# Gate and up products of a feed-forward layer by Strassen's scheme on one Trainium2 core: seven block products in place of eight

## Chip, cores and metric

The kernel runs on one core of one Trainium2 chip. The metric is the device time of one launch in microseconds. The core's engines are TensorE (PE, with its weight loads as PEld), VectorE (DVE), ScalarE (ACT), GpSimd (POOL) and SyncE (SP, which issues the DMAs).

## What is computed

Two transformer blocks of different kinds on a sequence of 512 tokens by 1024 features, in float32. The first block has two layers, and the change lies in the second half of each of them:

```python
h2 = rmsnorm(x, norm_ffn[l])
gu = jnp.einsum('btd,df->btf', h2, w_gate_up[l])      # 1024 -> 2 * 2816
g, up = jnp.split(gu, 2, axis=-1)
x = x + jnp.einsum('btf,fd->btd', jax.nn.silu(g) * up, w_down[l])
```

`rmsnorm` divides by the root of a token's mean square and multiplies by a gain per feature. Ahead of it in the layer stand the input projection, a sliding-window attention, a convolution branch and `w_out`, whose product is added to `x`.

## The kernel before

Activations lie with features on the 128 partitions and the 512 tokens along the free dimension, so `x` is eight tiles of 128x512 (`KT` = 8). `FF` = 2816 gives `FT` = 22 output tiles of gate and 22 of up. TensorE gets close to float32 by splitting each operand into a high part (a ScalarE copy to float32r) and a low part (a VectorE subtraction, source minus high), and `mm3` issues three matmuls for each product: high by high, low by high, high by low.

Weights come as chunks of 128x2048 float32 (1 MB) by SyncE into `w_raw`, which has two slots. `prep` of ScalarE (L523) makes `w_hi` of a whole chunk and `prep` of VectorE (L1071) makes `w_lo`. One chunk serves one pair of gate and up tiles: `pair` on TensorE computes the gate tile in PSUM bank `mm0` and the up tile in `mm1`, 8 contraction tiles x 3 matmuls of 128x512 each, 48 matmuls a pair and 22 pairs a layer. `gated` on VectorE takes both banks with the factor `rstd` (L1082, the token's inverse root), ScalarE applies SiLU (L777), VectorE multiplies (L1407) and the product is split into `act_hi` (L546) and `act_lo` (L1100) for the down product, 8 output tiles of 22 x 3 matmuls.

Ahead of gate and up, the `w_out` stage makes the eight tiles of `x`. For each, VectorE adds the bank to `x` (L1382), ScalarE makes `in_hi` and a square, VectorE makes `in_lo` (L1105), and GpSimd adds the square to `ssum` (L464) for the norm. The sum over partitions is two matmuls (`sum_halves`) inside the first pair; ScalarE then makes `rstd`.

The order on each engine is written out by hand. Engines wait for one another by counting semaphores; the layers and the pairs are hardware loops on every engine, with registers for the counts.

Of the kernel before, what the change touches and what calls it, by code (L numbers as in the profile page):

```python
# [54 lines left out]
SIGMOID = "sigmoid_and_others"  # L55

# [4 lines left out]
L_MM = 102  # L61
# [74 lines left out]
def program(nc, W, X, CONST, PARL, PARS, ROPE1, ROPE2, SGT, DIST, GOUT, OUT, strides):  # L136
    with ExitStack() as ctx:
# [43 lines left out]
        xh = sb("in_hi", [P, KT, T], F32R)  # L181
        xl = sb("in_lo", [P, KT, T], F32R)
        acth, actl = phase(("act_hi", [P, FT, T], F32R), ("act_lo", [P, FT, T], F32R))
        (ga, y, apad, qr, _, kd, _, va, _, pr, pt, _, rope1) = phase(
# [113 lines left out]
        s_one = sem("ones_ready")  # L298

# [37 lines left out]
        def _(e):  # L337
            L = Loops(e, "sp", strides)
            w_free, raw_q, k_in, k_turned = (L.count(s) for s in (s_w, s_qr, s_kr, s_kt))

# [37 lines left out]
            with L.loop(0, DEPTH) as l:  # L378
# [3 lines left out]
                e.wait_ge(s_in, l * (2 * KT) + KT)  # L382
# [21 lines left out]
                stage(n + (10 + QT), (L_UG + L_KV + L_QG + L_GB + L_CO + L_OUT + L_GU - 10 - QT) // 2)  # L404
                stage(n + (L_CHUNKS - L_DOWN), L_DOWN // 2, (HALF, HALF))
# [43 lines left out]
        def _(e):  # L449
# [3 lines left out]
            guess, scale = L.count(s_qx), L.count(s_qn)  # L453
            e.sem_inc(s_sum, 2)
# [35 lines left out]
            with L.loop(0, DEPTH) as l:  # L490
# [5 lines left out]
                add_squares()  # L496
                add_squares()
# [3 lines left out]
        def _(e):  # L501
# [6 lines left out]
            root, gel, par, r2 = L.count(s_rs), L.count(s_gel), L.count(s_par), L.count(s_r2)  # L508
            ogs, raw_q, means, guess, dens = (L.count(s) for s in (s_og, s_qr, s_hm, s_qx, s_rl))
# [139 lines left out]
            with L.loop(0, DEPTH) as l:  # L649
# [106 lines left out]
                with L.loop(0, L_OUT // 2) as i:  # L756
                    for c in range(2):
                        for d in range(2):
                            m = i * 4 + (2 * c + d)
                            tiles.skip(1)  # L760
                            if d:
                                prep(c)
                            e.wait_ge(s_sum, added.next())
                            e.wait_ge(s_mmf, taken.next())
                            hi(tile(xh, m), tile(x, m), col(parl, m + A_GF))
                            square(tile(x, m), d)
# [3 lines left out]
                inverse_root(tD[:], rstd[:])  # L770


                def gated(m, c, cols=CH):
                    tiles.skip(2)
                    prep(c, cols)
                    e.wait_ge(s_mmf, taken.next())
# [1639 lines left out]
```

## Time and profile before

| | |
|---|---|
| median of 3 runs | 2195.36 us (2194.89 to 2195.74) |
| the profiled execution | 2195.25 us, its span 2193.5 us |
| TensorE busy | 2181.2 us, 99% of the span |
| VectorE busy | 1377.9 us, 63% |
| ScalarE busy | 965.3 us, 44% |
| GpSimd busy | 74.8 us, 3% |
| gate and up, each layer | 240.2 us |

Matmuls are pipelined: the row of one shows from its start to its modelled end, and the next one starts before that. The rate of a stream is the distance from one start to the next. The same holds, to a smaller degree, for instructions of VectorE and ScalarE that stand back to back.

### The profile page before, as it was taken

The numbers are of one execution on the slowest core, as the hardware profiler recorded it, in microseconds if no ns is written. First come the engines' busy times: TensorE is split into PE (matmuls) and PEld (weight loads), VectorE is DVE, ScalarE is ACT, GpSimd is POOL, SyncE is SP. The second block draws the span as 40 slices with busy tenths as digits, with TensorE's granted clock in tenths as the row PEclk, the third lists the DMA queues.
The fourth block names the chain that finished last, engine by engine and source line by source line (L and its number), as shares of the span: only waits on it lengthen the run. The fifth ranks groups of instructions, "written<-read, shape, count | busy, mean of one in ns | idle before, by whom it ended". The sixth has DMA issues, their size and how long they took to land.

```text
span 2193.5 us, 28930 instructions
## 1 busy us (share of the span) xinstructions
PE 2181.2 (99%) x10528; PEld 1812.7 (83%) x10528; DVE 1377.9 (63%) x1978; ACT 965.3 (44%) x1392; POOL 74.8 (3%) x103
## 2 busy tenths in 40 slices
PE   9999999999999999999999999999999999999998
PEld 6878888888888878888888888888888899888887
DVE  8999944444335999954444334654776568888723
ACT  5678444443223588544343223332554344333412
POOL 0000020000010000020000010000000000000000
PEclk9999999999999999999999999999999999999999
DMA  5221222222223211222222224223222231222222
GB/s 188 69 81 61 97 96 96 96 96 84 93 94 122 90 62 65 94 96 99 98 98 94 81 92 152 100 78 128 82 96 88 97 135 39 103 99 99 92 96 77
DMA packets 35653, 208.39 MB, mean 95 GB/s; under 512 B 4512, under 2 KB 5024, under 8 KB 15072
## 3 DMA queue, kind: packets, MB, share of 16 engines
q1 hardware_dynamic: 35120, 206.43, 27.0%
q8 instruction: 60, 0.98, 0.2%
q10 hardware_dynamic: 432, 0.64, 0.1%
q14 instruction: 41, 0.34, 0.0%
HBM read 201.15 MB, written 2.10 MB: 93 GB/s over the span
## 4 chain that ended last, share of the span: by engine, by line
PE 94%; ACT 3%; DVE 2%; issue 1%; DMA 0%; SPq 0%; DVEq 0%; ACTq 0%
PE mm L1797 25%; PE mm L1799 25%; PE mm L1798 25%; PE sp L1799 4%; PE sp L1798 4%; PE sp L1797 4%; PE sp L1899 1%; PE ob L1927 1%; ACT probs L582 1%; DVE conv_y L1172 1%; DVE probs L1202 1%; ACT probs L590 1%; PE sp L1914 0%; DMA x<-in_x_dram 0%; PE ob L1799 0%
## 5 line engine op out<-in xcount | busy, mean ns | idle before, releaser
L1797 PE MATMUL mm<-in_hi,w_hi 128*128 128x512 f32 (+1 forms) x1696 | 663.5, 391 | 3.2 <-DVE w_lo L1071 1.6
L1799 PE MATMUL mm<-in_hi,w_lo 128*128 128x512 f32 (+1 forms) x1696 | 657.0, 387 | 0.0
L1798 PE MATMUL mm<-in_lo,w_hi 128*128 128x512 f32 (+1 forms) x1696 | 656.9, 387 | 0.0
L523 ACT ACTIVATE w_hi<-w_raw 128x2048 fp32r<-128x2048 f32 (+3 forms) x193 | 346.2, 1794 | 674.4 <-PE mm L1799 557.2
L1071 DVE TENSOR_TENSOR w_lo<-w_raw,w_hi 128x2048 fp32r<-128x2048 f32 (+3 forms) x193 | 422.2, 2188 | 240.2 <-ACT w_hi L523 239.8
L1797 PEld LDWEIGHTS mm<-in_hi,w_hi 128*128 128x128 f32 x1696 | 318.4, 188 | 74.4 <-issue 8.0
L1799 PEld LDWEIGHTS mm<-in_hi,w_lo 128*128 128x128 f32 x1696 | 318.4, 188 | 65.4
L1798 PEld LDWEIGHTS mm<-in_lo,w_hi 128*128 128x128 f32 x1696 | 318.6, 188 | 64.2 <-issue 1.0
L1172 DVE SCALAR_TENSOR_TENSOR conv_y<-conv_in,parl,conv_y 128x512 f32<-128x512 f32 x240 | 169.9, 746 | 1.7
L1082 DVE TENSOR_TENSOR tB<-mm,rstd 128x512 f32<-128x512 f32 x54 | 37.3, 690 | 172.8 <-PE mm L1799 172.8
L1797 PE MATMUL mm<-act_hi,w_hi 128*128 128x512 f32 x352 | 136.9, 389 | 0.0
L1798 PE MATMUL mm<-act_lo,w_hi 128*128 128x512 f32 x352 | 136.9, 389 | 0.0
L1799 PE MATMUL mm<-act_hi,w_lo 128*128 128x512 f32 x352 | 136.9, 389 | 0.0
L1797 PE MATMUL sp<-in_hi,w_hi 128*128 128x512 f32 (+1 forms) x256 | 96.8, 378 | 0.0
L1799 PE MATMUL sp<-in_hi,w_lo 128*128 128x512 f32 (+1 forms) x256 | 96.2, 376 | 0.0
L1798 PE MATMUL sp<-in_lo,w_hi 128*128 128x512 f32 (+1 forms) x256 | 96.2, 376 | 0.0
L464 POOL TENSOR_TENSOR ssum<-ssum,sq 128x512 f32<-128x512 f32 x28 | 54.8, 1957 | 881.4 <-ACT sq L549 881.4
L546 ACT ACTIVATE act_hi<-tD 128x512 f32 (+1 forms) x66 | 41.4, 628 | 87.9 <-DVE tD L1407 80.4
L1798 PEld LDWEIGHTS mm<-act_lo,w_hi 128*128 128x128 f32 x352 | 66.1, 188 | 13.8
L1797 PEld LDWEIGHTS mm<-act_hi,w_hi 128*128 128x128 f32 x352 | 66.1, 188 | 13.6
L1799 PEld LDWEIGHTS mm<-act_hi,w_lo 128*128 128x128 f32 x352 | 66.1, 188 | 13.6
L1100 DVE TENSOR_TENSOR act_lo<-tD,act_hi 128x512 f32 (+1 forms) x66 | 45.5, 689 | 41.1 <-ACT act_hi L546 41.1
(429 smaller groups left out, 3251.5 us busy)
## 6 DMA issues: line engine op xcount, KB each, us to landing
w_raw<-in_w_dram SPq DMA_DIRECT2D x160, 1024.0 KB, 4.8
w_raw<-in_w_dram SPq DMA_DIRECT2D x32, 704.0 KB, 3.9
w_raw<-in_w_dram SPq DMA_DIRECT2D x5, 512.0 KB, 4.5
out_dram<-z_rows SPq DMA_DIRECT2D x8, 256.0 KB, 2.1
rope<-in_rope_dram SPq DMA_DIRECT2D x3, 512.0 KB, 3.7
x<-in_x_dram SPq DMA_DIRECT2D x4, 256.0 KB, 4.8
x<-in_x_dram SPq DMA_DIRECT2D x2, 512.0 KB, 8.3
sq<-ssum SPq DMA_DIRECT2D x32, 32.0 KB, 1.8
```

The lines of the kernel that those rows point to most:

```text
L464: e.tensor_tensor(ssum[:], ssum[:], sq[:, k % 2, :], ALU.add).then_inc(s_sum, added.up())
L523: e.activation(whi[:, slot, 0:cols], raw[:, slot, 0:cols], ACT.Copy).then_inc(s_whi, whi_out.up())
L546: e.activation(dst, src, ACT.Copy, scale=scale).then_inc(s_fn, fn.up())
L582: last = e.activation(p, p, ACT.Exp, bias=ng[:, j:j + 1], accum_out=ls[:, j:j + 1])
L590: last = e.activation(p, p, ACT.Copy, scale=rl[:, 4 * h + n:4 * h + n + 1])
L1071: TT(wlo[:, slot, first:cols], raw[:, slot, first:cols], r32(whi[:, slot, first:cols]), ALU.subtract).then_inc(s_w, w_out.up())
L1082: TT(dst, four[bank], rstd[:] if op_in is None else op_in, ALU.mult).then_inc(s_mmf, taken.up())
L1100: TT(dst, src, r32(hi_), ALU.subtract).then_inc(told.sem, told.up())
L1172: STT(y[:, t, :], a, w, y[:, t, :], ALU.mult, ALU.add).then_inc(s_do, own.up())
L1797: MM(out, ah, bh, start=first, stop=False, **kw)
L1798: MM(out, ah, bl, start=False, stop=False, **kw)
L1799: return MM(out, al, bh, start=False, stop=last, **kw)
```

## The change

Gate and up of one tile are seen as a 2x2 block product: the rows of blocks are gate and up, the contraction of 1024 is cut in two halves of 512, and the 512 tokens are cut in two halves of 256. Winograd's form of Strassen's scheme gives the four result blocks from seven block products, each of 4 contraction tiles x 3 matmuls of 128x256: 84 of them for a pair. For this it needs

- four sums of token blocks (`T1` to `T4`), made once per layer while the `w_out` stage runs, with high and low parts of seven token operands of 4 tiles each;
- four sums of weight blocks (S1, S2, S4 and W21-W11) for every pair, three by GpSimd (`weight_sums`) and one by VectorE (`fourth_sum`), with high and low parts of seven weight operands of 128x512, each in its own `spot` of `w_hi` and `w_lo`;
- partial results that are used twice: ScalarE copies three half banks a pair out of PSUM (`copied_out`) and VectorE adds them to other banks (`take_product`).

The up half is no longer multiplied by `rstd`; in its place `down` multiplies its result by `rstd` before it is added to `x`. The first `KEPT` = 12 activation tiles lie where the first token operands also lie, so they are kept in float32 and split only at the end of the stage. The down product takes the tiles in the order 12 to 21, then 0 to 11. The loops of VectorE, ScalarE and GpSimd over layers and pairs are written out. TensorE still loops. The pieces of the diff are, in this order, GpSimd's, ScalarE's, VectorE's and TensorE's, and last the line of `down` on VectorE.

```diff
+    def weight_sums(a, fifth_done):
+        e.wait_ge(s_raw[a], raws[a].next(16))
+        e.wait_ge(s_sm, done.now(-fifth_done))
+        e.tensor_tensor(spot(wsum, 1), raw[:, a, A21], raw[:, a, A22], ALU.add).then_inc(s_su, made.up())
+        e.wait_ge(s_sm, done.now(-3))
+        e.wait_ge(s_su, made.now())
+        e.tensor_tensor(spot(wsum, 2), raw[:, a, A11], spot(wsum, 1),
+                        ALU.subtract).then_inc(s_su, made.up())
+        e.wait_ge(s_sm, done.now(-6))
+        e.tensor_tensor(spot(wsum, 4), raw[:, a, A21], raw[:, a, A11],
+                        ALU.subtract).then_inc(s_su, made.up())
+        done.skip(7)
...
-    def gated(m, c, cols=CH):
-        tiles.skip(2)
-        prep(c, cols)
-        e.wait_ge(s_mmf, taken.next())
-        e.activation(tC[:], tA[:, 0:T], ACT.Silu).then_inc(s_fn, fn.up())
-        taken.skip(1)
-        e.wait_ge(s_val, val.next())
-        hi(tile(acth, m), tD[:])
+    def gated_pair(p, m, split):
+        silu()
+        e.wait_ge(s_su, summed.next())
+        high_of_sum(4)
+        copied_out(copy_5[p % 2], bank_z[p % 2], 1)
+        e.wait_ge(s_sm, done.now(-2))
+        high_of(6, raw[:, p % 2, A22])
+        if split:
+            act_high(m)
+        copied_out(copy_2[p % 2], bank_x[p % 2], 3)
+        if p < FT - 1:
+            next_weights(p)
+            if p < FT - 2:
+                weights_beyond(p)
+            done.skip(7)
...
-    def gated(m, c, cols=CH):
-        take(tA[:, 0:T], 0)
-        take(tB[:, 0:T], 1)
-        prep(c, cols)
-        e.wait_ge(s_fn, fn.next())
-        e.wait_ge(s_mmf, taken.now())
-        TT(tD[:], tC[:], tB[:, 0:T], ALU.mult).then_inc(s_val, val.up())
-        lo(tile(actl, m), tD[:], tile(acth, m))
+    def gated_pair(p, m, split):
+        low_of_sum(4)
+        act_of(p - 1, m, 2, val if split else own, fn.next())
+        low_of(6, raw[:, p % 2, A22])
+        if split:
+            act_low(m)
+        upper_takes(p, 4)
+        lows_for_next(p)
+        lower_takes(p, (6, 7), p < FT - 2)
...
+            def gated_pair(p):
+                a = p % 2
+                e.wait_ge(s_sv, products.now(5))
+                operand(3)
+                times(bank_z[a], 1, T1, True)
+                e.wait_ge(s_sv, products.now(2))
+                times(bank_x[1 - a], 6, T4, False)
+                e.wait_ge(s_sc, copies.now(-1))
+                operand(4)
+                times(bank_x[a], 2, T2, False)
+                e.wait_ge(s_sv, products.now(3))
+                times(bank_y, 3, B21, True)
+                last = p == FT - 1
+                if not last:
+                    e.wait_ge(s_sv, products.now(0))
+                    operand(6)
+                    times(bank_x[1 - a], 0, B11, True)
+                e.wait_ge(s_sc, copies.now(-3))
+                operand(6 if last else 7)
+                times(bank_x[a], 4, T3, False)
+                e.wait_ge(s_sc, copies.now(-2))
+                operand(5)
+                times(bank_z[a], spot_s4(p), B22, False)
...
-                    TT(tile(x, m), mm[d][:], tile(x, m), ALU.add).then_inc(s_mmf, taken.up())
+                    scaled = (tA, tB)[d][:, 0:T]
+                    TT(scaled, mm[d][:], rstd[:], ALU.mult).then_inc(s_mmf, taken.up())
+                    e.wait_ge(s_mmf, taken.now())
+                    TT(tile(x, m), scaled, tile(x, m), ALU.add).then_inc(s_val, val.up())
```

Below, the seven products of a pair are called P1 to P7 in TensorE's order: T1 by S1, T4 by W22 (which ends the pair before), T2 by S2, B21 by W12, B11 by the next pair's W11, T3 by W21-W11, B22 by S4.

This is one pair of tiles on VectorE in the loop of gate and up, before (`mm` is a PSUM bank, the names after the arrow are inputs):

```order
839 L1082 TENSOR_TENSOR tA<-mm,rstd 128x512 [waits tile_ready]
840 L1081 REGISTER_ALU
841 L1082 TENSOR_TENSOR tB<-mm,rstd 128x512 [waits tile_ready]
842 L1070 ISA
843 L1071 TENSOR_TENSOR w_lo<-w_raw,w_hi 128x2048 [waits w_hi_ready]
844 L1405 ISA
845 L1406 ISA [waits scalar_value]
846 L1407 TENSOR_TENSOR tD<-tC,tB 128x512 [waits tile_taken]
```

And this is one pair on VectorE after, from the middle of the stage (`sp` is PSUM too, `sq` and `tD` hold ScalarE's copies):

```order
468 L1606 TENSOR_TENSOR w_lo<-w_raw,w_hi 128x512 [waits weight_operand_high]
469 L1687 TENSOR_TENSOR tA<-sp,tD 128x256 [waits product_copied,strassen_product_ready]
470 L1606 TENSOR_TENSOR w_lo<-w_raw,w_hi 128x512 [waits weight_operand_high]
471 L1672 TENSOR_TENSOR w_sum<-w_raw,w_sum 128x512 [waits weight_sum_by_pool]
472 L1606 TENSOR_TENSOR w_lo<-w_sum,w_hi 128x512 [waits weight_operand_high] x3
473 L1687 TENSOR_TENSOR tB<-mm,sq 128x256 [waits product_copied,strassen_product_ready]
474 L1687 TENSOR_TENSOR tA<-sp,sq 128x256 [waits product_copied,strassen_product_ready]
475 L1692 TENSOR_TENSOR tA<-tA,rstd 128x512 [waits product_taken]
476 L1606 TENSOR_TENSOR w_lo<-w_raw,w_hi 128x512 [waits weight_operand_high]
477 L1606 TENSOR_TENSOR w_lo<-w_sum,w_hi 128x512 [waits weight_operand_high]
478 L1698 TENSOR_TENSOR act<-mm,tC 128x256 [waits strassen_product_ready,scalar_value]
479 L1699 TENSOR_TENSOR act<-tB,tC 128x256
```

Four instructions and a split of the activation have become fourteen, and the split of the activation is a fifteenth where the tile is not kept.

On GpSimd nothing stood between the seven additions of squares of the `w_out` stage and those of the down stage. After, three sums for each of 21 pairs stand there:

```order
45 L530 TENSOR_TENSOR ssum<-ssum,sq 128x512 [waits square_ready,sum_zeroed]
46 L530 TENSOR_TENSOR ssum<-ssum,sq 128x512 [waits square_added,square_ready] x6
47 L571 TENSOR_TENSOR w_sum<-w_raw 128x512 [waits strassen_product_ready,raw_loaded1]
48 L574 TENSOR_TENSOR w_sum<-w_raw,w_sum 128x512 [waits weight_sum_by_pool,strassen_product_ready]
49 L577 TENSOR_TENSOR w_sum<-w_raw 128x512 [waits strassen_product_ready]
```

In the `w_out` stage VectorE had, for each tile of `x`, the addition and `in_lo`. After, this stands there for the sixth and the start of the seventh tile:

```order
426 L1606 TENSOR_TENSOR w_lo<-w_raw,w_hi 128x512 [waits weight_operand_high]
427 L1649 TENSOR_TENSOR w_sum<-w_raw 128x512
428 L1651 TENSOR_TENSOR w_sum<-w_raw,w_sum 128x512 [waits weight_sum_by_vector]
429 L1653 TENSOR_TENSOR tA<-w_raw,w_sum 128x512 [waits weight_sum_by_vector]
430 L1606 TENSOR_TENSOR w_lo<-w_sum,w_hi 128x512 [waits weight_operand_high] x2
431 L1606 TENSOR_TENSOR w_lo<-w_raw,w_hi 128x512 [waits weight_operand_high]
432 L1614 TENSOR_TENSOR x<-mm,x 128x512 [waits tile_ready]
433 L1630 SCALAR_TENSOR_TENSOR early<-early,parl,tB 128x256 [waits scalar_value]
434 L1631 SCALAR_TENSOR_TENSOR in_sum<-x,parl,tB 128x256
```

The first pair's weight work has moved ahead of the seventh tile's addition, and each of the last four tiles brings eight instructions of 128x256 in place of one of 128x512.

## Rows read from the trace of the kernel before

**Rows 1.** The page's busy times and instruction counts by engine.

```profile
PE 2181.2 (99%) x10528; PEld 1812.7 (83%) x10528; DVE 1377.9 (63%) x1978; ACT 965.3 (44%) x1392; POOL 74.8 (3%) x103
```

**Rows 2.** Busy time by stretch: `w_out`, gate and up, and down of layer 0.

```profile
core 0: us, PE busy (x) PEld busy (x) DVE busy (x) ACT busy (x) POOL busy (x), PEclk, DMA share, GB/s
272.10:315.60 43.50, 43.50 (x193) 36.03 (x192) 21.73 (x23) 17.01 (x20) 15.56 (x7) 1.00 0.29 104
315.60:555.80 240.20, 240.19 (x1060) 198.59 (x1060) 108.54 (x113) 96.94 (x90) 0.00 (x0) 1.00 0.27 92
555.80:675.70 119.90, 119.81 (x529) 98.92 (x527) 44.82 (x35) 31.82 (x33) 11.83 (x7) 1.00 0.29 96
```

**Rows 3.** Timeline: start, duration; first and 42nd matmul of a stream of 128x256.

```profile
1776.55 0.28 PE L1797 MATMUL mm<-in_hi,w_out 128*128 128x256 f32 x1
...
1781.40 0.28 PE L1799 MATMUL mm<-in_hi,w_out 128*128 128x256 f32 x1
```

**Rows 4.** Timeline of VectorE in gate and up; brackets: idle before, and releaser.

```profile
536.16 2.29 DVE L1071 TENSOR_TENSOR w_lo<-w_raw,w_hi 128x2048 fp32r<-128x2048 f32 x1 [1.26 <-ACT w_hi L523]
...
545.09 0.69 DVE L1082 TENSOR_TENSOR tB<-mm,rstd 128x512 f32<-128x512 f32 x1 [3.80 <-PE mm L1799]
546.50 1.62 DVE L1071 TENSOR_TENSOR w_lo<-w_raw,w_hi 128x1408 fp32r<-128x1408 f32 x1 [0.72 <-ACT w_hi L523]
```

**Rows 5.** Timeline of VectorE, instructions back to back in another stage.

```profile
250.26 0.69 DVE L1360 TENSOR_TENSOR conv_lo<-conv_y,conv_hi 128x512 fp32r<-128x512 f32 x1
250.87 0.68 DVE L1100 TENSOR_TENSOR conv_lo<-conv_y,conv_hi 128x512 fp32r<-128x512 f32 x1
...
253.28 0.69 DVE L1082 TENSOR_TENSOR tC<-mm,gate_b 128x512 f32<-128x512 f32 x1 [1.13 <-PE mm L1799]
254.01 0.69 DVE L1374 TENSOR_TENSOR tD<-tC,gate_a 128x512 f32<-128x512 f32 x1
```

**Rows 6.** VectorE by line and form: count, busy us, mean ns, idle before.

```profile
L1661 DVE TENSOR_TENSOR ssum<-ssum,sq 128x256 f32<-128x256 f32 x24 | 9.9, 417 | 0.3 <-ACT sq L954 0.3
L1679 DVE SCALAR_TENSOR_TENSOR in_lo<-x,pars,in_hi 128x256 fp32r<-128x256 f32 x16 | 7.6, 478 | 0.2 <-ACT in_hi L546 0.2
```

**Rows 7.** ScalarE by line and form, the same columns.

```profile
L546 ACT ACTIVATE act_hi<-tD 128x512 f32 x60 | 37.6, 627 | 78.7 <-DVE tD L1407 73.3 <-DVE tD L1738 5.4
L777 ACT ACT_TABLE_LOAD x20 | 25.7, 1283 | 0.4
L546 ACT ACTIVATE rv_hi<-og 128x256 fp32r<-128x256 f32 x16 | 5.7, 402 | 0.0
```

**Rows 8.** Timeline of VectorE at two additions of GpSimd.

```profile
286.43 2.28 DVE L1071 TENSOR_TENSOR w_lo<-w_raw,w_hi 128x2048 fp32r<-128x2048 f32 x1
288.64 0.69 DVE L1382 TENSOR_TENSOR x<-mm,x 128x512 f32<-128x512 f32 x1
...
603.01 0.75 DVE L1105 SCALAR_TENSOR_TENSOR in_lo<-x,parl,in_hi  x1 [1.35 <-ACT in_hi L546]
603.68 2.72 DVE L1071 TENSOR_TENSOR w_lo<-w_raw,w_hi 128x1408 fp32r<-128x1408 f32 x1
```

**Rows 9.** Timeline of GpSimd, these two additions.

```profile
286.41 3.45 POOL L464 TENSOR_TENSOR ssum<-ssum,sq 128x512 f32<-128x512 f32 x1 [4.18 <-ACT sq L549]
...
603.52 1.40 POOL L464 TENSOR_TENSOR ssum<-ssum,sq 128x512 f32<-128x512 f32 x1 [13.21 <-ACT sq L549]
```

**Rows 10.** Timeline of VectorE in the `w_out` stage: tiles 5, 6 and 7 of `x`.

```profile
304.96 0.69 DVE L1382 TENSOR_TENSOR x<-mm,x 128x512 f32<-128x512 f32 x1 [3.01 <-PE mm L1799]
...
310.40 0.69 DVE L1382 TENSOR_TENSOR x<-mm,x 128x512 f32<-128x512 f32 x1
...
315.84 0.69 DVE L1382 TENSOR_TENSOR x<-mm,x 128x512 f32<-128x512 f32 x1 [3.01 <-PE mm L1799]
```

**Rows 11.** The page's DMA issues: KB each, us from issue to landing.

```profile
w_raw<-in_w_dram SPq DMA_DIRECT2D x160, 1024.0 KB, 4.8
```

**Rows 12.** Longest of TensorE's waits, 33 to 315 us: total, times, longest.

```profile
PE sp L1914 <- ACT probs L590: 0.8, 3, 0.3
```

More of the change, by code:

```diff
@@ L55 @@
 SIGMOID = "sigmoid_and_others"
+SILU = "silu_and_others"
 L_UG, L_KV, L_QG, L_GB, L_CO, L_OUT, L_GU, L_DOWN = 4, 2, 8, 4, 2, 4, 22, 16
@@ L489, in _ @@
             added.skip(KT)
-            with L.loop(0, DEPTH) as l:
+            for l in range(0, DEPTH):
                 e.wait_ge(s_mmf, l * L_MM + 2)
@@ L647, in _ @@
             sum_hi()
-            with L.loop(0, DEPTH) as l:
+            for l in range(0, DEPTH):
                 e.preload_act_table_set(LN_EXP)
@@ L767, in _, with high_of, high_of_sum, copied_out @@
-                sum_hi()
+                def high_of(n, src):
+                    e.activation(spot(whi, n), src, ACT.Copy).then_inc(s_sh, high.up())
+                def high_of_sum(n):
+                    high_of(n, spot(wsum, n))
+                def copied_out(dst, src, product):
+                    e.wait_ge(s_sm, done.now(-product))
+                    e.activation(dst, src, ACT.Copy).then_inc(s_sc, copies.up())
+                def landed(slot):
+                    e.wait_ge(s_raw[slot], raws[slot].next(16))
@@ new lines, in token_high, with first_weights, first_sums @@
+                def token_high(o, k, src, scale=1.0):
+                    hi(token_operand(HIGH, o, k), src, scale)
+                def first_weights():
+                    landed(0)
+                    e.wait_ge(s_mm, tiles.now())
+                    high_of(0, raw[:, 0, A11])
+                def first_sums():
+                    for n in (1, 2):
+                        e.wait_ge(s_ds, sums.next())
+                        high_of_sum(n)
+                    high_of(3, raw[:, 0, A12])
@@ L782, in _, with prep_down @@
-                with L.loop(0, L_GU // 2 - 1) as i:
-                    gated(i * 2, 0)
-                    gated(i * 2 + 1, 1)
-                gated(FT - 2, 0, HALF)
-                gated(FT - 1, 1, HALF)
+                inverse_root(tC[:], rstd[:])
+                weights_beyond(0)
+                e.preload_act_table_set(SILU)
+                for p in range(1, FT):
+                    gated_pair(p, p - 1, p > KEPT)
+                def prep_down(slot, product):
+                    landed(slot)
+                    e.wait_ge(s_sm, done.now(-product))
+                    e.activation(whi[:, slot, 0:HALF], raw[:, slot, 0:HALF], ACT.Copy).then_inc(s_whi, whi_out.up())
@@ L937, in _ @@
                 ret_gate(2 + d, 1, d)
-            with L.loop(1, S_AR // 2) as i:
+            for i in range(1, S_AR // 2):
                 for c in range(2):
@@ L1174, in convolve @@
                 at[0] += count
-            with L.loop(0, DEPTH) as l:
+            for l in range(0, DEPTH):
                 input_norm(ems, zero=False)
@@ L1429, in down @@
                         prep(1, cols)
-                with L.loop(0, KT // 2 - 1) as i:
+                for i in range(0, KT // 2 - 1):
                     down(i * 2, 0)
@@ L1636, in _ @@
                 ret_gate(2 + d, 1, d)
-            with L.loop(1, S_AR // 2) as i:
+            for i in range(1, S_AR // 2):
                 for c in range(2):
@@ L1879, in two, with times @@
                         ins.then_inc(s_mm, tiles.up())
-                two(sub)
+                two((kept, sub))
                 with L.loop(1, KT // 2):
                     two(None)
+            def times(out, n, o, start, ready=None):
+                for k in range(HK):
+                    if ready is not None:
+                        e.wait_ge(s_cmb, combos.now(-ready(k)))
+                    a = slice(k * P, k * P + P)
+                    ins = mm3(out, spot(whi, n)[:, a], spot(wlo, n)[:, a], token_operand(HIGH, o, k),
+                              token_operand(LOW, o, k), start and k == 0, k == HK - 1, skip_group_check=True)
+                ins.then_inc(s_sm, done.up())
```

390 lines of the change are left out of this document (337 added, 53 removed).

## The prediction, made before the changed kernel ran

> **What bounds the kernel now.** The page comes first: TensorE is busy for 99% of the span, VectorE 63%, ScalarE 44%, GpSimd 3% [rows 1]. The stretches then show where: gate and up of one layer take 240.20 us, TensorE is busy in all of it at full clock, GpSimd does nothing there, and VectorE is busy for 108.54 us, under half [rows 2]. So time is won here by fewer columns through TensorE, as long as the others keep up. The timeline of VectorE shows how much room they have: in a pair it is idle 3.80 us before it takes the up bank [rows 4]. Last I read how GpSimd and VectorE meet in the two other stages [rows 8, 9], since the change puts both to work at once.
>
> **What TensorE saves.** 1060 matmuls in 240.20 us are 0.2266 us each [rows 2], so a pair of 48 takes 10.88 us. Matmuls of 128x256 in a stream start every (1781.40 - 1776.55)/41 = 0.1183 us [rows 3]. 84 of them are 9.94 us. The saving is 0.94 us a pair, 20.7 us a layer, 41.4 us in all, if nothing else ends later. The Trainium skill (TensorE: Matmul & The Clock Gate, "Back-to-back issue gap") gives a gap of N/2.4 + 2.5 ns, so 0.216 and 0.109 us; by it a pair would go from 10.36 to 9.17 us and save 1.19. The rows are slower at both widths, and I use them.
>
> **What VectorE must do.** Back to back, instructions of 128x512 start 0.61 us apart; one that reads what the one before wrote starts 0.73 us after it [rows 5]. One of 128x256 takes 0.417 us [rows 6], and less the same overlap of 0.08 it starts 0.34 apart. A pair needs seven low parts, one weight sum and the gate times `rstd`, nine of 128x512, 5.61 us with one dependence, and five of 128x256 (three takes, two for the activation), 1.72 us: 7.33 us. Where the activation is split in the pair (8 of 20 pairs), 7.94. Both are below 9.94.
>
> **What GpSimd adds.** It makes three sums of 128x512 a pair. Its addition at 286.41 took 3.45 us: VectorE's `w_lo` held it to 288.71, and it ended at 289.86, so 1.15 us of its own [rows 8, 9]. The addition at 603.52 began to run when `in_lo` ended at 603.76 and ended at 604.92; `w_lo` behind it took 2.72 us [rows 8, 9] where the same form takes 1.62 [rows 4], so VectorE lost 1.10. The addition `x<-mm,x`, with one input from PSUM, ran its usual 0.69 us beside GpSimd [rows 8]. So they exclude each other wherever VectorE reads two SBUF tensors, which is ten of its fourteen instructions. The Trainium skill (SBUF — State Buffer, on the shared port pair) calls this an exclusive lock held for a whole instruction. It speaks against the change: by it, three sums in a row with no gap give 7.33 + 3.45 = 10.78 us a pair, where TensorE alone needs 9.94. The trace agrees with the lock, and what is left to find is how much of the 3.45 falls beside PSUM instructions or gaps.
>
> **One pair, laid out.** TensorE's products end at 1.6, 3.0, 4.4, 5.8, 7.3, 8.7 and 10.1 us after the pair's start (1.42 each, with the last matmul's 0.28). VectorE can't begin the gate times `rstd` until P7 is taken. Then SiLU 0.63, the high part of W21-W11 0.54 behind it (ScalarE's 0.63 less overlap) [rows 7], its low part and the activation follow, and P5 of the next pair waits for that activation's read of its bank. Two sums of GpSimd (after P1 and after P3) fall into this chain, the third (after P6) into the low parts that P1 of the next pair waits for. I laid instruction behind instruction in this order, GpSimd going first where it asked first. The first sum is half covered by the take from PSUM or the wait for SiLU, the second by the first half of the activation, the third costs all of its 1.15. Adding some 0.6 us in which VectorE waits for SiLU and the high part, in kept pairs VectorE comes round in 10.2 to 10.4 us: I take **10.3**. With the split, 0.61 more and a wait for its high part: 11.0 to 11.4, **11.2**. TensorE waits for VectorE in both. Weights come in time: a slot is free about 3 us before the pair ends and the load takes 4.8 us [rows 11], so it lands some 2 us into the next pair, where the first sum wants it at 1.6 and the high part of W11 only after.
>
> **The start.** Take tile 5's product as time 0 (304.93); tiles come every 5.44 us [rows 10] and gate and up would start at 10.7. Tile 5 brings 0.69, eight STT or TT of 128x256 (0.40 and 0.34 apart [rows 6]) and 0.55 of waiting for ScalarE, 4.4 us; the first weights 4.5 us; GpSimd's addition of the square 1.1. So tile 6 is added at 9.9 instead of 5.5, and tile 7 at 14.2 instead of 10.9. Its token operands, with one addition of GpSimd and the first weight sum in the way, are ready at about 19.0, where P3 would end at 15.0. P5 then waits for a low part that stands behind them, to 22.3. The first pair, with the 0.95 us of `sum_halves`, ends at about 27.5 where it could at 21.6. In the second pair stand, in series, take, mean square, logarithm and exponential (0.63 each), `rstd` times gate, a table load of 1.28 [rows 7], SiLU and the low part, before P5: 2.6 us more. Two pairs of before end at 10.7 + 22.7 = 33.4, two of after at about 40.1: **6.7 us lost** in each layer.
>
> **The rest.** The second instruction of `down` (0.73 us per tile of 15 us) and the 12 late splits (0.61 each on VectorE, 0.54 on ScalarE, while TensorE spends 0.68 on each tile) lie under the down product, in which VectorE is busy 44.82 of 119.90 us [rows 2]; uncovered, the last tile's would cost 0.7 us a layer. Loops without registers can give back little: the largest wait of TensorE in the attention is 0.8 us a layer [rows 12]. I put both at nothing. The last pair has no P5 of a next one and a weight split between: 10.4.
>
> **The sum**, for one layer: +6.7 at the start; 11 kept pairs x (10.3 - 10.88) = -6.4; 8 split pairs x (11.2 - 10.88) = +2.6; last pair -0.5. That is +2.4, in two layers +4.8 us. The profiled execution took 2195.25 us, 0.1 from the median of the runs, so **2200 us**. With 0.2 us either way on the pairs and 2 on the start this case spans 2188 to 2212. Within 0.2% (4.4 us) two times can't be told apart here.
>
> **The rivals.**
> - *TensorE stays the bound.* GpSimd finds room beside VectorE, pairs take 9.94, and the start loses 4.4 without GpSimd's share. 4.4 - 19 x 0.94 - 0.9 is -14.4 a layer: **2166**. For it: 7.94 us of VectorE's work in 9.94. Against it: the full 1.10 that VectorE lost at 603.68 [rows 8]. Chance 0.18.
> - *Sums mostly in gaps.* GpSimd's requests meet the waits for SiLU and for P4 and P6 more often than I laid out: pairs 10.1 and 10.7, start 6.2. 6.2 - 8.6 - 1.4 - 0.7 is -4.5 a layer: **2186**. Chance 0.20.
> - *My case*, **2200**, chance 0.40.
> - *The chain to P5 closes* (slower). If the second sum asks just before the low part of W21-W11 instead of just behind it, which in my layout is a matter of 0.1 us, the activation is read 0.9 us after P5 wanted its bank, and the pair becomes 10.9, split 11.65; from a pair of 10.88 on, nothing is won at all. With 8 lost at the start: 8 + 0.2 + 6.2 is +14.4 a layer: **2224**. Chance 0.22.
>
> **How the numbers follow.** Faster by over 0.2% are the first two: 0.38. My case lies across the bound of 2199.8 and I give 0.14 of its 0.40 to no change and 0.26 to slower; with the last rival, slower is 0.48. The range takes most of the first and last case: 2168 to 2224.
>
> **What would show it.** In the profile after: matmuls of 128x256 at 0.118 us apart within a product, with TensorE's waits between products, on `act` or `w_lo`; VectorE busy 75 to 80% of gate and up; GpSimd's sums of 1.2 to 1.8 us and `w_lo` of 128x512 stretched from 0.69 to about 1.8 beside them; P3 of the first pair waiting 3 to 5 us. If TensorE has no waits in the middle of the stage, the first rival is right. If the waits are before P5, the last; before P1 and P2, mine. I would be wrong altogether if 256-wide matmuls that change PSUM bank every twelve were slower than the stream in [rows 3], or if ScalarE, with 11 or 12 instructions a pair, came late.

## The result, and the profile after

The changed kernel takes 2200.45 us (median of 8 runs, 2198.94 to 2203.09) where the kernel before, run beside it, takes 2195.41 (2194.89 to 2195.80). The ratio is 1.0024, 95% interval 1.0015 to 1.0034: slower by a quarter of a per cent, although TensorE now has 9% less to do in gate and up. Its profiled execution took 2199.27 us, with a span of 2197.5.

The page of the changed kernel: the busy times to hold against [rows 1], the chain that ended last, and two groups of VectorE's low parts (line, form, count, busy us, mean ns, idle before).

```profile
PE 2157.3 (98%) x12112; PEld 1862.3 (85%) x12112; DVE 1657.0 (75%) x2512; ACT 1048.0 (48%) x1789; POOL 266.8 (12%) x229
...
PE 71%; DVE 17%; ACT 5%; issue 4%; DMA 2%; SPq 0%; DVEq 0%
...
L1606 DVE TENSOR_TENSOR w_lo<-w_sum,w_hi 128x512 fp32r<-128x512 f32 x174 | 156.3, 938 | 18.6 <-ACT w_hi L851 18.6
...
L1606 DVE TENSOR_TENSOR w_lo<-w_raw,w_hi 128x512 fp32r<-128x512 f32 x132 | 115.5, 875 | 5.5 <-ACT w_hi L851 5.5
```

A low part of 128x512 takes 0.69 us in the kernel before [rows 5], and 0.88 (from `w_raw`) and 0.94 (from `w_sum`) on average here. The gate-up stages of both layers, as busy time by stretch, the columns as in [rows 2]:

```profile
315.14:557.43 242.29, 228.38 (x1852) 223.67 (x1851) 226.77 (x335) 134.61 (x270) 100.51 (x64) 0.99 0.27 94
981.21:1224.43 243.22, 228.35 (x1851) 223.41 (x1851) 227.39 (x335) 134.91 (x270) 99.95 (x64) 0.99 0.26 94
```

Against 240.20 us [rows 2] that is 2.1 and 3.0 more, where TensorE alone would need some 20 less. VectorE is busy for 94% of the stage. What TensorE waited for in the middle of it, 340 to 555 us (total, times, longest):

```profile
PE mm L2158 <- DVE tB L1687: 4.9, 8, 0.6
PE mm L2158 <- DVE act L1698: 4.4, 4, 1.6
```

A kept pair is one whose activation tile stays in float32 for the time being, a split pair one in which it is split. All of these waits are for VectorE. Those for `tB` (the product that must be taken before P2) are 0.61 or 0.62 us each, in seven of the 8 split pairs and in the last pair. Those for `act` stand before P5: the longest, 1.6 us, still belongs to the second pair, which ends at 344.1, and the three others are 0.96 us each, in three kept pairs. The first matmuls of P1 in the timeline give the length of each pair. Of the 11 kept pairs eight take 9.94 to 10.17, and three, every third or fourth, take 11.4. Such a long pair, first on VectorE, then GpSimd, ScalarE and TensorE (timeline: start, us, and in brackets the idle time before and what ended it):

```profile
365.93 1.73 DVE L1692 TENSOR_TENSOR tA<-tA,rstd 128x512 f32<-128x512 f32 x1
367.59 0.68 DVE L1606 TENSOR_TENSOR w_lo<-w_raw,w_hi 128x512 fp32r<-128x512 f32 x1
368.88 1.76 DVE L1606 TENSOR_TENSOR w_lo<-w_sum,w_hi 128x512 fp32r<-128x512 f32 x1 [0.62 <-ACT w_hi L851]
370.56 0.41 DVE L1698 TENSOR_TENSOR act<-mm,tC 128x256 f32<-128x256 f32 x1
...
365.83 1.28 POOL L571 TENSOR_TENSOR w_sum<-w_raw 128x512 f32<-128x512 f32 x1 [1.16 <-DMA w_raw<-in_w_dram]
368.81 1.28 POOL L574 TENSOR_TENSOR w_sum<-w_raw,w_sum 128x512 f32<-128x512 f32 x1 [1.70 <-PE mm L2160]
...
367.69 0.63 ACT L945 ACTIVATE tC<-tA 128x512 f32<-128x512 f32 x1 [1.27 <-DVE tA L1692]
368.23 0.61 ACT L851 ACTIVATE w_hi<-w_sum 128x512 fp32r<-128x512 f32 x1
...
369.87 0.28 PE L2160 MATMUL sp<-early_hi,w_lo 128*128 128x256 f32 x1
371.11 0.38 PE L2158 MATMUL mm<-in_hi,w_hi 128*128 128x256 f32 x1 [0.96 <-DVE act L1698]
```

Read it as a chain. GpSimd's first sum stretches the gate times `rstd` from 0.69 to 1.73 us. SiLU on ScalarE waits for it, and the high part of W21-W11 waits behind SiLU, though its input, GpSimd's third sum, was ready at 364.7 us. VectorE is idle for 0.62 us until that high part comes at 368.85. By then GpSimd's second sum is 0.07 us ahead, and the low part takes 1.76 us. The activation is read that much later. P5 starts 1.24 us after the matmul before it, where 0.12 is the distance in a stream: 1.1 us late.

A split pair, of which all but the first last 10.95 to 10.97 us, has the same idle time and three stretched instructions:

```profile
481.92 1.05 DVE L1692 TENSOR_TENSOR tA<-tA,rstd 128x512 f32<-128x512 f32 x1
...
484.19 0.69 DVE L1606 TENSOR_TENSOR w_lo<-w_sum,w_hi 128x512 fp32r<-128x512 f32 x1 [0.61 <-ACT w_hi L851]
...
485.13 1.23 DVE L1699 TENSOR_TENSOR act<-tB,tC 128x256 f32<-128x256 f32 x1
...
489.21 2.98 DVE L1606 TENSOR_TENSOR w_lo<-w_sum,w_hi 128x512 fp32r<-128x512 f32 x3
```

The first sum costs VectorE 0.36 us here, the second 0.81, and the third, in one of the three low parts of the last row, 1.09.

### The profile page after: what moved, and what is told of

Its sections match the earlier page's. It is cut to its first block, busy times and chain, and to the rows that moved or that the text cites. A ratio compares the mean times of both kernels' runs of the same rounds, so it can differ in the third digit from the quotient of the medians.

```text
span 2197.5 us, 31630 instructions
## 1 busy us (share of the span) xinstructions
PE 2157.3 (98%) x12112; PEld 1862.3 (85%) x12112; DVE 1657.0 (75%) x2512; ACT 1048.0 (48%) x1789; POOL 266.8 (12%) x229
## 4 chain that ended last, share of the span: by engine, by line
PE 71%; DVE 17%; ACT 5%; issue 4%; DMA 2%; SPq 0%; DVEq 0%
PE mm L2158 18%; PE mm L2160 17%; PE mm L2159 17%; DVE w_lo L1606 7%; PE sp L2160 4%; PE sp L2158 4%; PE sp L2159 4%; DMA w_raw<-in_w_dram 2%; DVE act L1699 1%; DVE tA L1692 1%; DVE conv_y L1386 1%; DVE tA L1687 1%; DVE w_sum L1672 1%; ACT w_hi L851 1%; DVE probs L1416 1%
## 5 line engine op out<-in xcount | busy, mean ns | idle before, releaser
L2158 PE MATMUL mm<-in_hi,w_hi 128*128 128x512 f32 (+1 forms) x1520 | 545.3, 359 | 24.9 <-DVE tB L1687 11.2
L2159 PE MATMUL mm<-in_lo,w_hi 128*128 128x512 f32 (+1 forms) x1520 | 532.6, 350 | 0.0
L2160 PE MATMUL mm<-in_hi,w_lo 128*128 128x512 f32 (+1 forms) x1520 | 532.5, 350 | 0.0
L616 ACT ACTIVATE w_hi<-w_raw 128x2048 fp32r<-128x2048 f32 (+3 forms) x145 | 256.2, 1767 | 461.4 <-PE mm L2160 343.4
L1285 DVE TENSOR_TENSOR w_lo<-w_raw,w_hi 128x2048 fp32r<-128x2048 f32 (+3 forms) x149 | 323.2, 2171 | 195.9 <-ACT w_hi L616 193.5
L1606 DVE TENSOR_TENSOR w_lo<-w_sum,w_hi 128x512 fp32r<-128x512 f32 x174 | 156.3, 938 | 18.6 <-ACT w_hi L851 18.6
L1606 DVE TENSOR_TENSOR w_lo<-w_raw,w_hi 128x512 fp32r<-128x512 f32 x132 | 115.5, 875 | 5.5 <-ACT w_hi L851 5.5
L851 ACT ACTIVATE w_hi<-w_sum 128x512 fp32r<-128x512 f32 x174 | 104.3, 621 | 18.2 <-DVE w_sum L1672 10.9
L2158 PE MATMUL sp<-early_hi,w_hi 128*128 128x256 f32 x352 | 100.2, 285 | 0.0
L2159 PE MATMUL sp<-early_lo,w_hi 128*128 128x256 f32 x352 | 100.2, 285 | 0.0
```

Of the source, the lines that this page charges most:

```text
L616: e.activation(whi[:, slot, 0:cols], raw[:, slot, 0:cols], ACT.Copy).then_inc(s_whi, whi_out.up())
L851: e.activation(spot(whi, n), src, ACT.Copy).then_inc(s_sh, high.up())
L1285: TT(wlo[:, slot, first:cols], raw[:, slot, first:cols], r32(whi[:, slot, first:cols]), ALU.subtract).then_inc(s_w, w_out.up())
L1606: TT(spot(wlo, n), src, r32(spot(whi, n)), ALU.subtract).then_inc(s_so, operands.up())
L2158: MM(out, ah, bh, start=first, stop=False, **kw)
L2159: MM(out, ah, bl, start=False, stop=False, **kw)
```

## Experiments

Each kernel was timed against the kernel before on the same chip, which took 2195.1 to 2195.4 us throughout. Times of pairs are worked out from the starts of P1 in the timeline of layer 0 (kept and split: the mean). e2 and e11 don't compute the products and serve only as measurements.

| kernel | us | ratio to before, 95% | first two pairs | kept (11) | split (8) | last |
|---|---|---|---|---|---|---|
| changed | 2200.45 | 1.0015 to 1.0034 | 28.96 | 10.38 | 10.86 | 12.23 |
| e1 sums on VectorE | 2200.04 | 1.0014 to 1.0032 | 30.24 | 10.20 | 11.09 | 12.18 |
| e2 fills for sums | 2163.99 | 0.9843 to 0.9873 | 26.23 | 9.94 | 9.94 | 10.43 |
| e3 second sum later | 2216.93 | 1.0086 to 1.0117 | 30.49 | 10.89 | 11.22 | 12.23 |
| e4 before, no loops | 2193.88 | 0.9985 to 1.0003 | | | | |
| e8 e1 + high part first | 2178.59 | 0.9909 to 0.9936 | 29.81 | 9.94 | 10.30 | 11.05 |
| e5 e8 + sums earlier | 2170.51 | 0.9873 to 0.9904 | 27.88 | 9.96 | 9.98 | 11.03 |
| e6 e5 + start, end | 2170.21 | 0.9871 to 0.9901 | 28.45 | 9.96 | 9.98 | 10.11 |
| e7 changed + start, end | 2196.28 | 0.9997 to 1.0015 | 27.66 | 10.38 | 11.01 | 11.19 |
| e9 e5 + root early, end | 2163.89 | 0.9841 to 0.9871 | 25.95 | 9.94 | 9.98 | 10.11 |
| e10 changed + high part first | 2185.36 | 0.9941 to 0.9968 | 28.43 | 10.15 | 10.63 | 10.83 |
| e11 one-input sums | 2166.95 | 0.9858 to 0.9889 | 27.57 | 9.94 | 9.94 | 10.59 |
| e12 e9 + copy of P1 early | 2164.71 | 0.9845 to 0.9878 | 26.22 | 9.94 | 9.98 | 10.11 |

**What GpSimd's sums cost.** First they go to VectorE, then they are replaced by something that reads nothing.

```diff
 # e1, VectorE
                         act_low(m)
+                    first_sum(p + 1)
                     upper_takes(p, 4)
...
                     low_of(3, raw[:, (p + 1) % 2, A12])
+                    second_sum(p + 1)
                     fourth_sum(p)
...
                     take_product(tB[:, 0:TH], bank_x[p % 2], copy_5[p % 2], seventh, 2)
+                    third_sum(p + 1)
```

> The changed kernel with the three weight sums of each pair on VectorE (in their places between its own instructions) and none on GpSimd in the gate-up stage. Theory A (a sum on GpSimd and a VectorE instruction that reads two SBUF operands run one after the other, so each sum takes its own 1.2 us from VectorE and comes late by what VectorE has already queued): VectorE has 7.33 + 3 x 0.65 = 9.3 us to do in a kept pair and 9.9 in a split one, all its own, against TensorE's 9.94; kept pairs 9.95 to 10.1 us instead of 10.38, split pairs 10.0 to 10.4 instead of 10.87, no wait of 1.24 us before P5 in every third pair; 4 to 8 us less per layer, 2184 to 2192 us in all. Theory B (VectorE is at its limit by the number of its own instructions and their order, and GpSimd's sums are mostly in its gaps): three more instructions a pair add up to 2 us to each of 19 pairs per layer, 2215 us or more.

```diff
 # e2, GpSimd, all three sums
-                    e.tensor_tensor(spot(wsum, 1), raw[:, a, A21], raw[:, a, A22], ALU.add).then_inc(s_su, made.up())
+                    e.memset(spot(wsum, 1), 0.0).then_inc(s_su, made.up())
...
```

> The changed kernel, where GpSimd's three sums per pair are replaced by fills with zero of the same 512 columns, with the same waits and signals; the sums of weight blocks are left out, so gate and up are not computed. Theory A (the cost is the shared reading of SBUF by two-operand instructions): a fill reads nothing, VectorE's low parts beside it stay at 0.6 us each and no sum is late; kept pairs 9.94 us, split pairs 9.94 to 10.2, 2174 to 2184 us in all. Theory B (the waits before P5 and P2 come from VectorE's and ScalarE's own orders or from the landing of the weights, whatever GpSimd does): pairs as they are, 2196 to 2202 us.

e2 came out 10 us below the range of theory A. It took 36 us off the changed kernel, and every pair from the third to the one before the last ran in 9.94 us. The fill took 0.53 us, and no instruction of VectorE was stretched beside one. So GpSimd's sums hold the pairs up; a fill is also shorter than a sum (0.53 against 1.28 us), and e2 alone doesn't part that from the reading. e11 below narrows it down. But e1, which takes the sums off GpSimd too, won nothing, and neither theory had its number. VectorE by group in e1, 340 to 555 us (the last columns are the idle time before and its releaser):

```profile
L1582 DVE TENSOR_TENSOR w_lo<-w_sum,w_hi 128x512 fp32r<-128x512 f32 x80 | 51.6, 686 | 13.0 <-ACT w_hi L826 13.0
L1582 DVE TENSOR_TENSOR w_lo<-w_raw,w_hi 128x512 fp32r<-128x512 f32 x60 | 41.2, 686 | 7.2 <-ACT w_hi L826 7.2
```

No low part is stretched any more, but VectorE is idle for 20.2 us in these 20 pairs, 0.65 and 0.36 us in each, waiting for high parts of ScalarE. With 9.9 us of its own work (split) that makes 10.9 of the 11.09 measured. In e2 VectorE waits as long for the same high parts (12.7 and 6.4 us over the same stretch), but there it has three instructions less to do in a pair and makes up for it. The idle time costs only where VectorE is full.

**The same two edits, singly and together.** Two lines of ScalarE are swapped, in e1 (e8) and in the changed kernel (e10).

```diff
-                    silu()
                     e.wait_ge(s_su, summed.next())
                     high_of_sum(4)
+                    silu()
```

> The kernel with all three sums on VectorE, where ScalarE also makes the high part of W21-W11 ahead of the pair's silu and not behind it. In the run without this VectorE was idle 0.62 us a pair, waiting for that high part, 0.36 us for the high part of W12 and 0.1 to 0.2 us otherwise, on 9.3 us (kept) or 9.9 us (split) of its own work; periods of 10.30 and 11.09 us. If those waits are the rest of the period (VectorE's chain sets it): 9.94 us in kept pairs, 10.5 in split ones, 8 to 9 us less per layer, 2181 to 2185 us. If the period comes from the chain over TensorE's products and the copies, whatever VectorE's own waits: 2198 to 2202 us.

> The changed kernel, its sums on GpSimd, with ScalarE's high part of W21-W11 ahead of silu and nothing else: the edit that took 21 us from the kernel with its sums on VectorE. If GpSimd's sums are what holds VectorE up (it has no idle time before that low part in the changed kernel, since a stretched instruction stands ahead of it): 2198 to 2201 us, no change. If the place of the high part is what costs in the changed kernel too: kept pairs near 9.94 and split ones near 10.4, 2185 us or less.

e8 came out 2.4 us under its range, with kept pairs at 9.94 and split ones at 10.30. In e10 the second case came, 0.4 us above its bound and with longer pairs than it said, 10.15 and 10.63. The premise of the first case was wrong: VectorE does have idle time there, the 0.62 us in the rows above. The swap alone takes 15 us off, where moving all sums alone takes off 0.4.

| us | SiLU first | high part first |
|---|---|---|
| sums on GpSimd | 2200.45 | 2185.36 |
| sums on VectorE | 2200.04 | 2178.59 |

The timeline of e10 in the pair that answers to the one above:

```profile
365.94 1.73 DVE L1692 TENSOR_TENSOR tA<-tA,rstd 128x512 f32<-128x512 f32 x1
367.60 0.68 DVE L1606 TENSOR_TENSOR w_lo<-w_raw,w_hi 128x512 fp32r<-128x512 f32 x1
368.20 0.68 DVE L1606 TENSOR_TENSOR w_lo<-w_sum,w_hi 128x512 fp32r<-128x512 f32 x1
368.81 0.41 DVE L1698 TENSOR_TENSOR act<-mm,tC 128x256 f32<-128x256 f32 x1
369.14 1.25 DVE L1699 TENSOR_TENSOR act<-tB,tC 128x256 f32<-128x256 f32 x1
```

The first sum stretches the gate exactly as before, but the high part is there and the low part gets in ahead of the second sum, which now stretches the second half of the activation, behind the read that P5 waits for. That read comes at 368.81 and not at 370.56. The sums cost VectorE no less (54.8 us over 340 to 555 us, against 48.8 in the changed kernel, counted as under e11 below). What is gone is its idle time before this low part, and with it the waits before P5 of kept pairs; those before P2 shrink from 4.9 to 2.8 us.

**Where the second sum falls.**

```diff
 # e3, GpSimd, before the second sum
                     e.wait_ge(s_su, made.now())
+                    if q > 1:
+                        e.wait_ge(s_so, lows.now(-7 * q))
```

> The changed kernel, where GpSimd's second sum of each pair from the third on also waits until VectorE has finished the low part of W21-W11 of the pair before. If the waits of 1.24 us before P5 in every third kept pair come from the second sum asking less than 0.1 us ahead of that low part and holding it up: they vanish, kept pairs 10.0 to 10.2 us instead of 10.38, split pairs as before, 2190 to 2196 us. If they come from the landing of weights or from ScalarE: still there, 2199 to 2202. If the sum made later is itself late for the next P1 or P3: new waits there, 2202 or more.

The wait for `act` before P5 did vanish past the second pair, but the third outcome came: TensorE waited up to 0.6 us for `w_lo` before P1 in nine pairs of the layer and up to 0.6 for `tB` in ten, 2217 us. This run shows that this delay of GpSimd's sum is no cure: the sum is late for what follows it.

**Early sums.** e5 is e8 with VectorE's second and fourth sum ahead of the take of P4 and no longer between the low parts.

```diff
                     first_sum(p + 1)
+                    e.wait_ge(s_sm, done.now(-3))
+                    second_sum(p + 1)
+                    fourth_sum(p)
                     upper_takes(p, 4)
...
                     low_of(3, raw[:, (p + 1) % 2, A12])
-                    second_sum(p + 1)
-                    fourth_sum(p)
                     low_of_sum(1)
```

> As the run before, and VectorE also makes the second and the fourth sum ahead of taking the fourth product, so that it doesn't stand idle for the high part of W12. VectorE's chain sets the period: 0.36 us less in split pairs, 10.0 to 10.2 us against TensorE's 9.94, kept pairs 9.94; 2175 to 2179 us. If TensorE's products set it: the time of the run before, 2181 to 2185 or 2200. If the early sums make the take of the fourth product late and with it P4 and P5: 2185 or more.

2170.5, some 5 us under the range: it also gave 2 us a layer at the start, which I hadn't counted. VectorE's groups in e5, same stretch:

```profile
L1582 DVE TENSOR_TENSOR w_lo<-w_sum,w_hi 128x512 fp32r<-128x512 f32 x80 | 51.4, 684 | 0.0
L1582 DVE TENSOR_TENSOR w_lo<-w_raw,w_hi 128x512 fp32r<-128x512 f32 x59 | 40.3, 683 | 0.0
```

The 20 us that VectorE waited for high parts in e1 are gone (the swap took 13.0 of them, the early sums the rest), and with them TensorE's waits in this stretch but for 0.6 us.

**One input instead of two.** In e11 each sum on GpSimd reads one block.

```diff
-                    e.tensor_tensor(spot(wsum, 1), raw[:, a, A21], raw[:, a, A22], ALU.add).then_inc(s_su, made.up())
+                    e.tensor_scalar(spot(wsum, 1), raw[:, a, A21], 2.0, 0.0, ALU.mult, ALU.add).then_inc(s_su, made.up())
...
```

> The changed kernel, where each of GpSimd's sums reads one block only (twice that block, 512 columns, same waits and signals); the sums of weight blocks are left out, so gate and up are not computed. If what holds VectorE up is two instructions with two SBUF inputs each at once: VectorE's low parts stay at 0.6 us each and the time is that of the fills, 2164 to 2168 us. If any GpSimd instruction that reads SBUF holds it up: 2180 us or more, with low parts of 1.2 us or longer beside it.

The instruction of GpSimd takes 0.88 us on average, two thirds more than the fill. The time is that of the first theory, its reason is not quite: a VectorE instruction beside such a one still takes up to 1.10 us instead of 0.69. Over 340 to 555 us such excess (over 0.685 us for 128x512 and 0.417 for 128x256) is 9.7 us in 27 instructions, where it is 48.8 us in 58 in the changed kernel. There are 58 sums in both: VectorE loses 0.84 us on average to one with two inputs, 0.17 to one with one, and nothing to a fill (e2).

**Start and end.** e6 and e7 make the same edits to e5 and to the changed kernel: ScalarE copies the first product ahead of tile 7, the third sum stands behind tile 7, VectorE adds the last three squares itself, and at the end the product for P7 is taken ahead of the low parts for down.

```diff
                 upper_takes(FT - 1, 4)
-                prep(0, HALF)
...
-                kept_low(0)
                 take_product(tB[:, 0:TH], bank_x[1], copy_5[1], 5, 2)
+                prep(0, HALF)
                 take_product(tA[:, TH:T], bank_z[1], copy_2[1], 6, 3)
                 copies.skip(3)
                 scaled_gate()
+                kept_low(0)
                 kept_low(1)
```

> As the run before, with the start and the end of the stage changed too: at the start ScalarE copies the first product ahead of tile 7, VectorE makes the third sum behind tile 7 and adds the last three squares itself, so that GpSimd adds none beside it; at the end VectorE takes the product for P7 ahead of the low parts for down. If the wait of 2.5 us before P3 comes from the copy's place and the wait behind it from GpSimd's additions stretching VectorE: P3 begins 2 us earlier, 1.5 to 3 us less per layer; the end gives 1.0 us per layer. 2168 to 2173 us. If the start is bound by VectorE's own forms between tiles 6 and 7: only the end's 2 us, 2174 to 2176.

> The changed kernel with the same edits at the start and the end of the stage and nothing else; the sums stay on GpSimd. Start 1.5 to 3 us and end 1.0 us per layer, 2192 to 2196 us; if the granted clock no longer falls in the first pair, 3 us per layer more, 2187 to 2191. If the start is bound by VectorE's own forms: 2198.

The end gives its 0.9 to 1.0 us a layer in both. The start gives 1.3 us in e7 and loses 0.6 to 2.0 in e6. The squares cost VectorE 0.6 us each where it is already behind, which I had left out; that they are the whole of the loss isn't shown, since e12 below loses 0.2 to 0.3 without them. So e6 is within its range (2170.21) by luck: it was to gain at the start and lost. e7 is 0.3 us above its range. Its condition for 3 us more a layer, a clock that doesn't fall, came in layer 0, and the 3 us did not (last section). e9 therefore keeps only the end, and makes the root of the mean square earlier:

```diff
 # e9, VectorE
                     low_of_sum(1)
+                    if p == 0:
+                        mean_square(D, tC[:])
                     low_of_sum(2)
...
 # e9, ScalarE
+                e.preload_act_table_set(LN_EXP)
                 next_weights(0)
                 done.skip(7)
-                e.preload_act_table_set(LN_EXP)
```

> The fastest so far (sums early on VectorE, high part ahead of silu) with two more edits: at the end of the stage VectorE takes the product for P7 ahead of the low parts for down, and in the first pair the mean of squares is made by VectorE amid the low parts, with ScalarE's table for the root loaded ahead of the next pair's high parts. The wait of 0.9 us before the last P7 should go: 1.8 us in all. If the wait of 2.2 us before P5 of the second pair comes from the late root (its Ln began 333.9 us into the run, 2.0 us after the table for it), it shrinks to under 0.5: 3 to 4 us in all, 2164 to 2166. If that wait comes from VectorE's own queue there, the root is hidden: 2168 to 2169.

ScalarE in e5 (first fence) and in e9 (second), where logarithm, root and the next table are:

```profile
333.69 0.63 ACT L608 ACTIVATE tC<-tC 128x512 f32<-128x512 f32 x1 [1.97 <-DVE tC L1277]
334.36 0.63 ACT L611 ACTIVATE rstd<-tC 128x512 f32<-128x512 f32 x1
...
337.36 0.61 ACT L920 ACTIVATE tC<-tA 128x512 f32<-128x512 f32 x1
```

```profile
331.11 0.63 ACT L608 ACTIVATE tC<-tC 128x512 f32<-128x512 f32 x1 [0.79 <-DVE tC L1277]
331.77 0.63 ACT L611 ACTIVATE rstd<-tC 128x512 f32<-128x512 f32 x1
...
334.77 0.62 ACT L920 ACTIVATE tC<-tA 128x512 f32<-128x512 f32 x1
```

The root comes 2.6 us earlier, SiLU too, and the second pair takes 10.76 us where it took 12.56. At 2163.9 us this is the fastest kernel that computes the result: 1.4% under the kernel before.

> The kernel at 2163.9 us with two more edits in the first pair: ScalarE copies the first product ahead of tile 7 and VectorE makes the third sum behind tile 7's operands. P3 waited 2.4 to 2.5 us for the copy; its last quarter needs an operand of tile 7, which VectorE finished 322.2 us into the run and would finish 0.6 to 1.1 us earlier. If that operand ends the wait next: P3's first nine matmuls run 2 us earlier, its last three 0.6 to 1.1 us earlier, 0.5 to 1 us per layer, 2161.9 to 2163. If VectorE's queue behind it sets the second pair's start: unchanged, 2163.5 to 2164.3. If the granted clock falls for longer since TensorE now does its little work in two pieces: 2164.5 or more.

e12 was no faster (2164.71). The last quarter of P3 starts at 321.61 us and not at 322.26, but P5 then waits 0.9 us, P1 of the second pair 0.9 where it waited 0.3, and the second pair starts no earlier. That is the mechanism of the second case. The time is 0.4 us above its range and within that of the third, whose mechanism didn't come: the clock doesn't fall at all.

**Loops.** e4 is the kernel before with the loops of the three engines written out.

> The kernel before with the loops of ScalarE, VectorE and GpSimd written out as in the change, and nothing else. If the 1.3 us that the changed kernel's profile is shorter outside the gate-up and down stages come from this part: 2193.5 to 2194.7 us, 1.3 less than before. If they come from the other parts or are chance: 2195.2 to 2195.6, the time of before.

2193.88 (2193.47 to 2194.54, 11 runs) against 2195.14 (2194.68 to 2195.65, 21 runs) is 1.26 us less. The ranges do not overlap, but the interval of the ratio includes 1, so the size is uncertain.

## Why the prediction was right, and where it was not

The forecast was 2200.0, the time 2200.45. The steps:

- *What TensorE saves*: right. Pairs without a wait take 9.94 us.
- *The start, 6.7 us lost a layer* (two pairs in 29.4): 28.96, so 0.4 less. P3 waited twice, 2.4 and 1.6 us, together within the 3 to 5. The `sum_halves`, taken at 0.95 us, are two matmuls that take 0.47.
- *Kept pairs 10.3*: 10.38 and, in layer 1, 10.49; 0.9 and 2.1 us more a layer. VectorE's rounds, from one gate times `rstd` to the next, are the 10.2 us of the layout in most pairs and 11.0 in four of the 11, which the layout didn't have. And TensorE doesn't wait in each pair before P1 or P2, as forecast. It runs at 9.94 to 10.17 until VectorE is too late, and then waits once, before P5.
- *Split pairs 11.2*: 10.86 and 10.83. This term was mis-sized, by 2.7 and 3.0 us a layer. The prices of the sums were about right: 0.36, 0.81 and 1.09 us measured, where I charged the third its full 1.15 and the others about a half. With 0.75 us idle and the 7.94 of its own work VectorE comes round in 10.96, just under the 11.0 to 11.4 that I gave: the wait for the split's high part is 0.1 us, and I had allowed more. And in the first split pair TensorE hardly waits yet, it takes 10.17 (9.94 in layer 1).
- *The last pair 10.4*: 12.23. Mis-sized by 1.8 us. It left out that VectorE makes low parts for down ahead of the product that the last P7 needs; e6, e7 and e9 moved them and won 0.9 to 1.0. It also left out that VectorE is still late from the pairs before. By the starts of the matmuls the 2.3 us above 9.94 are 0.9 before P2 (for the take of `tB`), 0.4 for a copy by ScalarE and 1.0 before the last P7. With the low parts where they were, the pair takes 10.83 in e10 and 10.43 in e2.
- *Loops at nothing*: they give some 1.26 us (e4), about what the changed kernel's span gains outside gate and up: 5.1 lost inside, 4.0 in all.

The errors of the kept pairs, the split pairs, the last pair and the loops nearly cancel, so the half microsecond is luck: single terms were off by up to 3 us a layer. The main mechanism was right: GpSimd's sums and VectorE's two-input instructions exclude each other, and VectorE sets the pace. e2 and e11 show it, and put its price at 33 to 36 us with ScalarE's order as it is. By the signs that the prediction gave, waits before P2 in the split pairs speak for my case, and waits before P5 in the kept pairs for the last rival. That rival's mechanism, the second sum 0.1 us ahead of the low part of W21-W11, strikes in 7 of the 22 kept pairs. The cases weren't as separate as I had made them.

Two things the prediction did not see. It expected VectorE to be busy for 75 to 80% of the stage and it was 94%, since an instruction that is held up counts as busy: 48.8 of the 202.4 busy us between 340 and 555 us are such excess. And it took ScalarE's order as given: "SiLU 0.63, the high part of W21-W11 0.54 behind it". The high part doesn't need SiLU's result, and the table above puts the price of this order at 15 us with the sums on GpSimd and 21 with them on VectorE. So the change is slower than before by two things together, the sums on GpSimd and the place of one high part. With the high part first and all the rest as it is, e10 is 0.5% faster than before. With this order, moving the sums to VectorE does not help (e1), and only a GpSimd that reads one block does: e11 is 1.3% faster, though without the right sums.

What stays open: what sets how often a long kept pair comes (mostly every third), and how the root applied to the down output would do alone. The down stage takes 119.8 us from its first matmul to its last in both kernels, so no cost of it shows.

## What to carry to other kernels

Work handed to an idle engine isn't free if both engines read two SBUF tensors: here the sums on GpSimd took 0.84 us each from VectorE on average, which makes such a sum itself in 0.61 to 0.68. Before moving work, look on each engine for instructions whose input is ready but which stand behind one whose input is late; here swapping two lines was worth 15 to 21 us, and choosing the engine of the sums 0.4 to 7. And try such edits together as well as singly, since e1 alone would have said that the engine of the sums does not matter, and with the high part first it is worth 6.8 us.

## What the runs showed of the hardware

TensorE's granted clock fell in the first pair. Busy time by stretch in the changed kernel; the column before the last two is the granted clock:

```profile
315.00:318.00 3.00, 3.00 (x26) 2.90 (x24) 2.58 (x7) 2.85 (x7) 0.00 (x0) 1.00 0.03 5
318.00:321.00 3.00, 0.74 (x6) 0.57 (x5) 3.00 (x5) 1.25 (x4) 2.85 (x2) 1.00 0.00 0
321.00:323.00 2.00, 0.76 (x7) 0.55 (x5) 2.00 (x5) 1.39 (x4) 0.30 (x1) 0.78 0.00 0
323.00:325.00 2.00, 1.84 (x8) 1.84 (x9) 2.00 (x6) 2.00 (x5) 0.75 (x1) 0.50 0.00 0
325.00:327.00 2.00, 2.00 (x12) 2.00 (x11) 2.00 (x4) 2.00 (x6) 2.00 (x1) 0.50 0.01 4
...
329.00:331.00 2.00, 2.00 (x17) 1.91 (x16) 2.00 (x4) 1.74 (x4) 0.31 (x1) 1.00 0.96 311
```

From 318 to 323 us TensorE was busy for 1.5 of 5 us, and in the last part of them the granted clock fell to half (1.2 GHz). From 323.2 on matmuls of 128x256 came 0.213 us apart, 26 of them, and 6 us later they ran at full speed (2.4 GHz) again. In e12, where P3 starts earlier and in two pieces, TensorE is busy for 3.9 of the 7 us from 318 to 325, and the clock stays at full speed:

```profile
318.00:321.00 3.00, 1.38 (x10) 1.13 (x9) 2.42 (x6) 2.06 (x6) 1.48 (x1) 1.00 0.00 0
321.00:323.00 2.00, 1.39 (x11) 1.40 (x12) 2.00 (x6) 1.98 (x5) 0.00 (x0) 1.00 0.00 0
323.00:325.00 2.00, 1.09 (x9) 0.89 (x8) 2.00 (x5) 1.74 (x4) 0.00 (x0) 1.00 0.01 4
```

Yet e12 is no faster than e9, whose clock fell for about 12 matmuls a layer. e7 has both cases in one run. In layer 0 (the first two rows) the clock stays, in layer 1 (the last two) it falls, and the first two pairs take 27.66 and 27.69 us:

```profile
321.00:323.00 2.00, 1.07 (x9) 1.07 (x10) 2.00 (x7) 2.00 (x5) 0.37 (x1) 1.00 0.00 0
323.00:325.00 2.00, 0.97 (x9) 0.77 (x7) 1.90 (x3) 0.86 (x3) 2.00 (x1) 1.00 0.01 4
...
987.00:989.00 2.00, 2.00 (x11) 2.00 (x12) 2.00 (x5) 0.99 (x2) 1.22 (x1) 0.54 0.00 0
989.00:991.00 2.00, 1.26 (x6) 0.96 (x5) 1.90 (x3) 1.08 (x3) 1.24 (x1) 0.61 0.00 0
```

So the slow clock cost nothing there: VectorE was late anyway, and the slow matmuls lay under its work.
